# One quarter of a projection's weight units as seven block products in place of eight, in a one-core decoder layer

## The reference

```
h    = rms_norm(x, norm_mix)                      # (256, 2048)
proj = h @ w_in                                   # (2048, 3904): c_q 512 | c_kv 256 + k_pe 64 | q_sb 1024 | k_sb 1024 | v_sb 1024
q, k_nope, v_mla = from rms_norm(c_q) @ w_q_b and rms_norm(c_kv) @ w_kv_b, rotary on q_pe and k_pe
o    = [MLA softmax attention, 8 heads | stick-breaking attention of q_sb, k_sb, v_sb, 8 heads]
x    = x + concat(rms_norm(o_A), rms_norm(o_B)) @ w_out
x    = x + cross attention of rms_norm(x) into rms_norm(mem), 256 memory tokens, 4 heads
x    = x + mixture of 32 experts (2048 -> 512 -> 2048), top 1 group, top 2 experts in it
y    = rms_norm(x, norm_final)
```

## Time and profile before

| | us |
|---|---|
| median of 3 runs (lowest, highest) | 1349.26 (1348.88, 1350.79) |
| the profiled execution, its own time | 1352.07 |
| its span, first to last instruction | 1350.3 |
| granted TensorE clock, mean | 0.873 |

### The profile page before, as it was taken

The page is one execution under the profiler, slowest core; times in us unless marked ns, Lnnn a source line. Parts: engine busy times, 40 slices in busy tenths (PEclk is TensorE's granted clock), DMA queues, the critical chain, the costliest instruction groups (busy, mean ns, idle before and its releaser), DMA issues.

```text
span 1350.3 us, 20613 instructions
## 1 busy us (share of the span) xinstructions
PE 993.5 (74%) x8488; PEld 594.6 (44%) x8488; DVE 582.9 (43%) x1141; ACT 305.7 (23%) x549; POOL 42.7 (3%) x96
## 2 busy tenths in 40 slices
PE   8999999999999975666555666645566655566656
PEld 7888888888888522222222222212222222222222
DVE  5546587877656643233322233332233332223323
ACT  5664567774544100000000000000000000000002
POOL 1300000130000000000000000000000000000001
PEclk9999999999999997777877778787787787777879
DMA  7797864448769999999999999999999999999997
GB/s 243 224 229 259 246 187 129 152 150 292 276 234 363 350 419 427 433 430 432 433 433 431 431 431 433 433 431 431 431 433 433 431 432 430 433 433 431 432 424 302
DMA packets 79012, 486.40 MB, mean 360 GB/s; under 512 B 10183, under 2 KB 25661, under 8 KB 66046
## 3 DMA queue, kind: packets, MB, share of 16 engines
q1 hardware_dynamic: 78748, 485.56, 89.9%
q0 software_dynamic: 192, 0.31, 0.2%
q10 hardware_dynamic: 34, 0.01, 0.0%
HBM read 481.14 MB, written 4.72 MB: 360 GB/s over the span
## 4 chain that ended last, share of the span: by engine, by line
PE 48%; DMA 47%; SPq 2%; DVE 1%; issue 1%; ACT 1%; DVEq 0%; ACTq 0%
DMA gu<-in_w_up 42%; PE ps L1069 10%; PE ps L620 7%; PE ps L622 7%; PE ps L621 7%; PE ps L1124 5%; DMA down<-in_w_down 4%; PE ps L1048 2%; PE ps L1081 1%; DMA spill<-nat 1%; DMA w_raw<-in_w_in 1%; PE ps L867 1%; PE ps L869 1%; PE ps L868 1%; PE ps L600 1%
## 5 line engine op out<-in xcount | busy, mean ns | idle before, releaser
L1069 PE MATMUL ps<-gu,xe 128*32 128x256 f32 x3968 | 287.4, 454 | 304.8 <-DMA gu<-in_w_up 304.3
L2191 DVE TENSOR_TENSOR x_sum<-ps,x_sum 128x512 f32<-128x512 f32 x240 | 149.0, 683 | 508.6 <-PE ps L1081 508.6
L1069 PEld LDWEIGHTS ps<-gu,xe 128*32 128x32 f32 x3968 | 140.8, 130 | 469.0 <-DMA gu<-in_w_up 327.5
L1642 DVE TENSOR_TENSOR w_lo<-w_raw,w_hi 128x1024 fp32r<-128x1024 f32 (+1 forms) x137 | 164.3, 1209 | 109.5 <-ACT w_hi L1242 106.1
L620 PE MATMUL ps<-w_hi,a_hi 128*128 128x512 f32 (+1 forms) x468 | 183.5, 392 | 0.3 <-ACT w_hi L1242 0.3
L621 PE MATMUL ps<-w_lo,a_hi 128*128 128x512 f32 (+1 forms) x468 | 179.7, 384 | 0.0
L622 PE MATMUL ps<-w_hi,a_lo 128*128 128x512 f32 (+1 forms) x460 | 176.8, 384 | 0.0
L1242 ACT ACTIVATE w_hi<-w_raw 128x1024 fp32r<-128x1024 f32 (+1 forms) x137 | 141.6, 1040 | 124.4 <-PE ps L622 73.5
L1561 ACT ACTIVATE sg<-ps 128x128 f32<-128x128 f32 x31 | 8.6, 278 | 654.4 <-PE ps L1069 654.4
L1124 PE MATMUL ps<-down,act_t 128*32 128x512 f32 x976 | 112.5, 601 | 6.1 <-DMA down<-in_w_down 6.1
L620 PEld LDWEIGHTS ps<-w_hi,a_hi 128*128 128x128 f32 x468 | 87.9, 188 | 17.0 <-issue 0.7
(11 more groups left out here) (342 smaller groups left out, 837.4 us busy)
## 6 DMA issues: line engine op xcount, KB each, us to landing
down<-in_w_down SPq DMA_DIRECT2D x29, 4096.0 KB, 22.6
gu<-in_w_gate SPq DMA_DIRECT2D x28, 4096.0 KB, 31.6
gu<-in_w_up SPq DMA_DIRECT2D x28, 4096.0 KB, 40.9
w_raw<-in_w_in SPq DMA_DIRECT2D x56, 512.0 KB, 5.2
w_raw<-in_w_out SPq DMA_DIRECT2D x32, 512.0 KB, 4.4
gu<-in_w_up SPq DMA_DIRECT2D x18, 512.0 KB, 6.5
w_raw<-in_w_mem_kv SPq DMA_DIRECT2D x16, 512.0 KB, 3.4
down<-in_w_down SPq DMA_DIRECT2D x13, 512.0 KB, 16.0
```

Source lines behind the costliest of these rows:

```text
L1069: mm = pe.matmul(ps[5][j * SLOTS:(j + 1) * SLOTS, 0:2 * P].rearrange("s (m f) -> s m f", m=2), xe[:, k, :], gu[side][:, :, k, j * P:(j + 1 ...
L1642: ve.tensor_tensor(w_lo[:, u % RING, :, 0:n], w_raw[:, u % RING, :, 0:n], w_hi[:, u % RING, :, 0:n], ALU.subtract).then_inc(S("w_split"), 1)
L2191: ins = ve.tensor_tensor(x_sum[:, t, cols], ps[g][:, :], (x_res if first else x_sum)[:, t, cols], ALU.add)
```

## The change

In the four chunks `SB_Q` and `SB_K` (`SEVENS`), units `i` = 1 and 5 (`SEVEN_AT`) are taken as a 2 x 2 by 2 x 2 block product (two row tiles, two weight blocks, two column halves of 256) with seven products in place of eight. Three of them use the unit's own weights, at the unit's place. Four use sums of weights, and stand behind the unit two places later (`SEVEN_LAG`). Each product is three matmuls of 256 columns (`triple`), 21 in place of 12 of 512 columns. A chunk has four PSUM banks in place of two.

POOL makes the weight sums (`sum_weights`, three operations a unit) from `w_raw`, ACT rounds them (`t_hi`), DVE splits them (`t_lo`); `t_raw`, `t_hi`, `t_lo` have two buffers. The sums of row blocks (`s_sum`, `s_raw`, `s_hi`, `s_lo`) are made once, in chunk `KV_LAT`. When a chunk is done, DVE adds the products (`sum_sevens`, ten operations of 128x256), and ACT copies from that sum, three units later than before. `MOVE_AT` becomes 35, 43, 51, 59. `MEM_AT` becomes 35 to 38 and 59 to 62; ACT's squares of the first half move behind the copy of chunk 5, `turn_mem` of the first half into chunk 6, behind the split of unit 56, the second half's behind the split of unit 64. The rotary angles move behind `KV_LAT`, the latents' turns into `SB_K`'s chunks at `i` = 5. Semaphores with new names do what the old ones did.

```diff
-MEM_AT = [START[_c] + 3 + _q for _c in (SB_Q + 1, SB_V) for _q in range(NJ)]
+MEM_AT = [START[_c] + 3 + _q for _c in (SB_K, SB_V + 1) for _q in range(NJ)]
-MOVE_AT = [DONE[_c] + RING + 3 for _c in QUADS]
+MOVE_AT = [DONE[_c] + RING + (3 if _c == MEM_K else 7) for _c in QUADS]
+SEVENS = [SB_Q, SB_Q + 1, SB_K, SB_K + 1]
+SEVEN_AT, SEVEN_LAG = [1, 5], 2
...
 # SP, ahead of the load of unit u
                 if u >= RING:
                     sp.wait_ge(S("w_split"), u - RING + 1)
+                    if seven_of(u - RING) is not None:
+                        sp.wait_ge(S("t_summed"), seven_of(u - RING) + 1)
...
 # PE, project_sevens: what replaces project_units in the four chunks
+                    if i in SEVEN_AT:
+                        m = SEVEN_AT.index(i)
+                        triple(ps[b + 2][:, left], a11h, a11l, wh[:, 0, right], wl[:, 0, right], start=m == 0)
+                        triple(ps[b][:, right], a12h, a12l, wh[:, 1, right], wl[:, 1, right])
+                        triple(ps[b][:, left], s_hi[:, m, 3], s_lo[:, m, 3], wh[:, 1, left], wl[:, 1, left]
+                               ).then_inc(S("w_used"), 1)
...
+                    n = summed_of(u)
+                    if n is not None:
+                        pe.wait_ge(S("t_rounded"), n + 2)
+                        pe.wait_ge(S("t_split"), n + 3)
+                        for g, (dst, xh, xl) in enumerate((
+                                (ps[b + 2][:, right], s_hi[:, m, 0], s_lo[:, m, 0]),
+                                (ps[b + 3][:, right], s_hi[:, m, 2], s_lo[:, m, 2]),
+                                (ps[b + 3][:, left], s_hi[:, m, 1], s_lo[:, m, 1]),
+                                (ps[b + 1][:, right], a_hi[:, k, rows[1]], a_lo[:, k, rows[1]]))):
+                            cols = slice(g * HN, (g + 1) * HN)
+                            mm = triple(dst, xh, xl, th[:, cols], tl[:, cols], start=m == 0 and g == 1,
+                                        stop=last and g != 1)
+                        mm.then_inc(S("t_used"), 1)
...
 # ACT, the loop over the chunks of w_in
+                if c == SB_V + 1:
+                    rounded(START[c] + RING + 4)
+                    mem_squares(1)
...
-                rounded(DONE[c] + RING)
+                rounded(DONE[c] + RING + (3 if c in SEVENS else 0))
...
-                if c in (SB_Q + 1, SB_V):
-                    mem_squares((SB_Q + 1, SB_V).index(c))
                 if c == SB_K + 1:
+                    mem_squares(0)
...
 # DVE, the loop over the chunks of w_in
-                if c in (SB_K, SB_V + 1):
-                    split_w(START[c] + RING + 3)
-                    turn_mem((SB_K, SB_V + 1).index(c))
+                if c in (SB_V, SB_V + 1):
+                    split_w(START[c] + RING + 5)
+                    turn_mem(c - SB_V)
...
                 split_w(DONE[c] + RING)
+                if c in SEVENS:
+                    sum_sevens(c)
+                    split_w(DONE[c] + RING + 3)
                 if SB_Q <= c - 1 < SB_V:
                     turn_quads(QUADS.index(c - 1))
...
 # POOL, sum_weights
+                    gp.wait_ge(S(f"w_loaded{u % RING}"), 16 * (u // RING + 1))
+                    if m >= 2:
+                        gp.wait_ge(S("t_used"), m - 1)
+                    link(gp.tensor_tensor(t[:, 0:2 * HN].rearrange("p (h n) -> p h n", h=2),
+                                          w_raw[:, u % RING, :, 0:HN], two[:, ::-1], ALU.subtract))
+                    link(gp.tensor_tensor(t[:, 2 * HN:3 * HN], q[:, 2 * HN:3 * HN], t[:, 0:HN], ALU.subtract))
+                    gp.tensor_tensor(t[:, 3 * HN:4 * HN], q[:, 3 * HN:4 * HN], t[:, 2 * HN:3 * HN],
+                                     ALU.subtract).then_inc(S("t_summed"), 1)
```

More of the change, by code:

```diff
@@ L56 @@
 UN = 512
+HN = UN // 2
 Q_LAT, KV_LAT, SB_Q, SB_K, SB_V, Q_PE, Q_NOPE, K_NOPE, V_MLA = 0, 1, 2, 4, 6, 8, 9, 11, 13
@@ L1641, in split_w @@
                     ve.wait_ge(S("w_rounded"), u + 1)
+                    if seven_of(u) is not None:
+                        ve.tensor_tensor(plain_cols(w_lo, u), plain_cols(w_raw, u), plain_cols(w_hi, u),
+                                         ALU.subtract).then_inc(S("w_split"), 1)
+                        continue
                     ve.tensor_tensor(w_lo[:, u % RING, :, 0:n], w_raw[:, u % RING, :, 0:n],
@@ L1727, in _ @@
             split_w(DONE[Q_LAT] + RING)
[L1728 to L1745, removed]
-            link(ve.tensor_scalar(turns[:, :, :], turns[:, :, :], -magic, None, ALU.add))
-            for cc in (c1, c2, c3):
-                link(ve.scalar_tensor_tensor(out=ang, in0=turns[:, :, :], scalar=-cc, in1=ang,
-                                             op0=ALU.mult, op1=ALU.add))
@@ new lines, in _, with rotary_angles @@
+            from math import pi
+            import numpy as np
+            magic = 1.5 * 2.0 ** 23
+            half = ROPE // 2
+            def rotary_angles():
+                inv = small[:, 0:half]
+                pf = small[:, 32:34]
+                ve.wait_ge(S("consts"), 2)
+                ve.wait_ge(S("pos_loaded"), 16 * TT)
+                link(ve.tensor_copy(pf, pos_i[:, :]))
+                turns = place("rope_turns", [P, TT, ROPE // 2], offset=e_at + 85 * 1024)
+                for t in range(TT):
+                    ins = ve.tensor_scalar(rope_cs[:, 1, t, :], inv, pf[:, t:t + 1], None, ALU.mult)
+                link(ins)
+                c1 = 6.28125
+                c2 = float(np.float32(2 * pi - c1))
+                c3 = 2 * pi - c1 - c2
+                ang, cosv = rope_cs[:, 1], rope_cs[:, 0]
+                link(ve.tensor_scalar(turns[:, :, :], ang, 1.0 / (2 * pi), magic, ALU.mult, ALU.add))
+                link(ve.tensor_scalar(turns[:, :, :], turns[:, :, :], -magic, None, ALU.add))
+                for cc in (c1, c2, c3):
+                    link(ve.scalar_tensor_tensor(out=ang, in0=turns[:, :, :], scalar=-cc, in1=ang,
+                                                 op0=ALU.mult, op1=ALU.add))
+                link(ve.tensor_scalar(cosv, ang, pi / 2, None, ALU.add))
+                link(ve.tensor_scalar(turns[:, :, :], cosv, pi, -2 * pi, ALU.is_gt, ALU.mult))
+                link(ve.tensor_tensor(cosv, cosv, turns[:, :, :], ALU.add))
+                ve.tensor_scalar(rope_cs[:, :, :, :], rope_cs[:, :, :, :], 3.1415925, -3.1415925, ALU.min,
+                                 ALU.max).then_inc(S("angles"), 1)
```

234 lines of the change are left out of this document (188 added, 46 removed).

## The result

| kernel | median us | lowest to highest | runs | ratio to before, 95% interval |
|---|---|---|---|---|
| before, beside it | 1350.78 | 1348.88 to 1351.32 | 5 | |
| changed | 1366.03 | 1362.79 to 1370.05 | 5 | 1.0123, 1.0099 to 1.0147 |

The change costs 15 us where +6.0 was forecast and 1361 was the end of the range. The profiled execution of the changed kernel is its fastest, 1362.79, 10.7 above the one of before.

What follows compares the result with a forecast made beforehand. PE was taken to bound the kernel to some 447 us, then mostly expert-weight loads. Terms -2.0 - 0.3 + 1.5 + 4.4 + 2.4 = +6.0 us gave a median of 1355.3 us; range 1347.5 to 1361, the forecast's own 1352 to 1360.

Steps and rivals of the forecast that it cites:

- What it adds off PE, at no cost by itself: Row sums, weight sums, DVE's additions and the moves at units 43 and 51, on DVE, POOL, ACT and SP: 0.
- Does PE come back at full clock?: PE behind the stall at unit 60: clock stays full, 0; other end +1 (2 us at half rate).
- Gain: PE, eight treated units: 21 matmuls of 256 columns take 0.25 us less than a full unit, saving 2.0 us.
- the wait at unit 32: PE's wait behind the first move of a chunk goes, as the move now stands elsewhere: -0.3 us.
- the products are dearer: Rival: 256-column matmuls with changing weights above 0.1295 us, no gain, 1357.3; chance 0.12 shared with DVE's rival, above 1360.
- Row sums: Six DVE operations and one rounding in KV_LAT, hidden by four units split ahead: 0 (4.4 us without that lead).
- The moves at units 43 and 51: Each move takes 15.7 us of 20.4 available, and fits even with the longest write, 10.92 us: 0.
- First late load: Units 36 to 39, behind the first move and memory DMAs: loads of 38 and 39 late, +1.5 us (ends 0, 3.8).
- Unit 60: Load held behind SP's wait for transposes at unit 59 and the last move: +4.4 us (ends +0.6, some +10).
- Unit 65: DVE turns memory's second half between the splits of units 64 and 65: +2.4 us, 0 if unit 60 is in time.
- The lead holds: Rival: unit 60's load issued early enough, no stall there, 1347.0 us; chance 0.30 for holding or nearly so, 1346.6 to 1352.
- DVE becomes the bound: Rival: POOL's sums stop DVE in treated chunks, +11 in four chunks, 1367; chance 0.12 shared with dearer products, above 1360.

Runs made afterwards that it cites:

- I: H with DVE's row sums two units earlier in the latent chunk and the rotary angles behind them: 1348.66 us, ratio 0.9999.
- L: C with the row sums two units earlier, memory otherwise staged as in the changed kernel: 1357.21 us, ratio 1.0057.
- A: Changed kernel with the rotary angles back ahead of the row sums in the latent chunk: 1362.29 us, ratio 1.0085.
- D: Changed kernel with POOL's weight sums replaced by writes of zeros: 1358.32 us, ratio 1.0058.
- B: Changed kernel with the four DMAs of memory's second half one unit later, behind units 60 to 63: 1361.82 us, ratio 1.0091.
- C: Changed kernel with both edits, rotary angles back and memory's second half one unit later: 1358.99 us, ratio 1.0060.
- F: C with the second half's four memory DMAs at a sixteenth of their columns: 1352.26 us, ratio 1.0015.
- K: J with POOL's weight sums replaced by writes of zeros: 1349.19 us, ratio 0.9995.
- J: I with memory's eight squares and eight transposes one by one behind units' roundings or splits: 1349.19 us, ratio 0.9994.
- H: A with memory in two places of its own, its eight DMAs behind every second unit from 20 to 34: 1356.16 us, ratio 1.0042.
- E: Kernel before, without products, with only the changed kernel's schedule of memory DMAs, moves, squares and transposes: 1355.74 us, ratio 1.0038.

## Why the prediction was wrong, point by point

The direction and the place of the largest term were right, and SP's wait stood there; but what its loss hangs on was only half seen, as the point on unit 60 says. The sum was +6.0, and PE lost 13.75 from unit 12 to 66. The steps that failed are "What it adds off PE, at no cost by itself", with the angles' move, which I had not priced, and "Does PE come back at full clock?": 7.2 of the 7.7 us.

- *Gain*, -2.0 and -0.3 for the wait at unit 32: -2.17 in I. Of before's chunk 24-32, 0.47 was the late unit 32; the products save 0.4 a chunk, 1.6 in all, in place of 2.0 (half a chunk takes 2.74, 1.07, 2.75 and 4.13 us in I, 10.69 where I had 10.63). The price a 256-column matmul, 0.118 us, was right; "the products are dearer" falls.
- *Row sums*, 0 (end 4.4): +1.6 in 12-16, gone in I. "Four units split ahead" was false there: DVE waited for ACT's roundings four times in that chunk, 6.1 us, so it had no units ahead. The chunk sums, 4.8 us a chunk by the earlier trace rows, are nine operations of 0.42, not ten, 3.6 us, and cost nothing in I. The weight sums took POOL 2.9 to 5.2 us a unit, not 3.0. The moves at units 43 and 51, also put at 0, cost 0.3 together here (40-48 and 48-59 against I); in L, where PE came earlier, 1.4 and 1.1. That they fit with the longest write was wrong: L's took 6.6 and 7.5 us.
- *The rotary angles* were in the diff, behind `KV_LAT` on DVE, and appear in no term. They cost the wait at unit 20: 2.1 us against I's spacing, and 1.7 of half clock behind it; A takes back 3.85. Beside POOL's sums they took 5.1 us, without them 3.5 (D).
- *First late load*, +1.5: +0.83 (0.45 against I's -0.38), but +2.4 in A (2.02 + 0.38). The late PE hid part of it.
- *Unit 60*, +4.4: 5.54. From PE's start on unit 48 (140.80) the transposes ended 23.2 us on, not 20.6, as unit 54's load was late behind the move before it and ACT's copy and squares with it; the write took 4.7, not 7.2; the load took 5.6 to ACT, not 3.96, with memory in flight; DVE's turn of the moved chunk was done before the split, 0 and not 0.7. Four errors of 0.7 to 2.6 us, two of the other sign: that the term came near is in part luck. I had also said that units 61 to 63 come 2.79 apart, from rows of another place; B and C show 3.5 to 4.2. That matters more than the wait: with SP's wait gone, 59-66 still cost 8.1 and 9.3 us (B, C), and with a sixteenth of memory's bytes 0.2 (F). The sum had the wait in it, and put memory's bytes behind unit 60 at next to nothing (2.79 against 2.72 a unit).
- *Unit 65*, +2.4: 1.9, the transposes between the splits, as forecast.
- *Clock after a wait*, 0 (end +1): 1.7 behind unit 20, 1.8 behind unit 60. I chose the wrong one of two rows, though a wait doesn't always cost the clock (last section). The Trainium skill, "TensorE: Matmul & The Clock Gate", section "HAM oscillation — how this bites in real kernels", had the array come back cold behind a wait for a load; by that rule my sum was +7.0. The trace agrees with it at unit 60, where 1.8 us went, and shows the same at unit 20 behind a wait of 1.95 us for a split, not for a load.
- *Rivals.* "The lead holds" falls. "DVE becomes the bound" falls as a bound (I, K), but its mechanism was at work where the lead was thin: in D the stretch 16-24 costs 3.0 us less. The Trainium skill, "SBUF — State Buffer", section "Who interferes with whom", states the exclusion; the lengthening agrees in kind, with 1424 against 1239 ns a split.
- The sum of PE's terms, 13.75, stands for 15 us of median. The rest, and why the changed kernel's runs span 7 us, I can't assign: only one execution of each is profiled. That J's profiled run, the longest, waited behind moves where I's, the fastest, waited for no unit speaks for the moves' writes, but that is argued, not shown.

## What to carry to other kernels

Every operation that a diff moves needs its own line in the sum, on the engine that it is moved to, ahead of the unit that stands behind it there; small ones most of all. Where a kernel lives on a lead of a few units, count what each chunk's slack must pay (a move's hold, extra bytes at the rate measured where such pieces go beside the loads, a lump of transposes) and let no two fall in the same chunk. A saving of 2 us on the bound engine is worth less than one lost lead, which can cost the clock as well. And taking away the wait that ends last shows what stood behind it: only a run without it tells what it was worth.

## What the hardware showed that I had not expected

- Waits of one length did and did not cost the clock. Behind a wait of 1.95 us (unit 20, changed kernel) the granted clock fell to 0.50 for some 3 us, once PE had resumed; behind 1.68 (unit 20, B) and 1.77 (unit 56, H) it stayed at 1.00. Behind 1.93 us at its start unit 65 took 2.87 us in E, and 4.42 in C, where units 61 to 64 had waited too. At unit 60 the clock was 0.50 for a stretch behind a wait of 2.51 us in E, and stayed at 1.00 behind 2.50 in D.
- DMA share doesn't tell the rate: 1.09 at 194 GB/s in C, with weights and memory's pieces in flight (these land on 32 partitions each), and 0.94 at 302 in F, with a sixteenth of memory's bytes. Whether the partitions are the reason no run shows.
- The write of one chunk, 512 KB, took 4.7 to 10.9 us over the traces of before and after. What was in flight differed from one to the next; no run shows which of it counts.
